# Four first-branch gate products moved from the S5 half steps to the Hyena convolutions of a hybrid block

## The chip, the cores and the metric

The kernel runs on one core of a Trainium2 chip. The metric is the device time of one execution in microseconds (us). The engines are named as in the profile: TensorE (PE; PEld is its weight load), VectorE (DVE), ScalarE (ACT), GpSimd (POOL) and SyncE (SP), which here only issues loads and stores.

## The reference

One layer of a diffusion backbone: 512 latent tokens and 256 context tokens, width 1024. The normalised, modulated tokens h are projected by one wide matrix to the inputs of three token mixers and to the merge gates. The parts that matter here, cut from the reference:

```
h = rmsnorm(x) * (1 + sc1) + sh1
k_l, v_l, a_l, u_l, q_l, r_l, hy_l, gate_l = split_cols(h @ w_in, COL_SIZES)
...
y_hy  = x2 * long_conv_bidir(x1 * long_conv_bidir(v, h0, h1), h2, h3)     # branch 0, two convolutions
y_gla = gated linear attention readout                                    # branch 1
y_s5  = s5_readout(s5_bidir(u_l ...))                                     # branch 2, complex diagonal states
m = sigmoid(g_hy) * (y_hy @ w_hy) + sigmoid(g_gla) * (y_gla @ w_gla) + sigmoid(g_s5) * (y_s5 @ w_s5)
x = x + gt1 * (m @ w_out)
x = x + gt2 * swiglu(rmsnorm(x) * (1 + sc2) + sh2)
```

All of it is float32. The S5 branch has 32 groups of channels; both directions are computed, and each block of four groups and one direction is a unit of work below.

## The kernel before

The order of the work is one list, STEPS, written out by hand (lines 366 to 595). Each engine walks the same list and does its own part of each step, in order, so a step that one engine waits in holds back all that stands behind it on that engine. Weights go through a ring of four slots of 1 MB: `want` puts a load into a plan, SP issues the loads in the plan's order, and load n is issued only when the last step that uses load n - 4 is done on PE. Weights of projections are used as a sum of two parts: ACT copies the rounded part (`split`, L1394) and POOL subtracts it (L1239), four pieces for each 1 MB block; a program places each block's split between the steps at the earliest place at which its two-slot ring is free.

A projection product (`merge_g`, `hy`) is 128 output channels by 512 tokens with 8 blocks of depth, each times three pairs of parts: 24 matmuls, at L695. A branch product (`merge_b`) is 4 plain float32 matmuls, which the trace shows as 8 records. Eight PSUM banks are used in turn: a product waits until the product eight before it has been evicted.

- `merge_g` of branch 0 ("kept" gates, k0 to k7): ACT takes the sigmoid and writes it to DRAM (`gate_spill`); it is read back behind the second convolution (POOL's `yinv`, L1299). DVE has no part in it.
- `merge_g` of branches 1 and 2 (g): ACT takes the sigmoid (`gate_ev`, L1560).
- `merge_b` (b): DVE multiplies by the gate and, for branch 2, adds into the sum (`merge_ev`, L2102, L2107).
- `hy` (h0 to h11): ACT scales (L1508), DVE adds the two neighbours of the short filter (`hy_ev`, L2120, L2121).

**S5's half steps** (lines 513 to 532). m runs from 0 to 15, two for each of 8 blocks. In half step m DVE turns the states of m (`s5_r`, with a scan at L2051), adds the kernel products of m + 1 (`s5_ka`, L2067 or L2069), turns back (`s5_x`, L2080 to L2083), makes the angles and factors of m + 2 (`s5_gen`, L1993 to L2008) and of its output (`s5_v`, L2021 to L2024). PE does the state products of m + 1 (`s5_d`, L919), in even half steps from 2 on the output products of the block before (`s5_y`, L945, L950), the transposes (`s5_w`, L906) and the kernel products of m + 2 (`s5_k`, L931), which wait for `s5_v`. `s5_v` of blocks 2 and up waits for the output products two blocks before. The last block's outputs stand behind half step 15. Two places in each half step take a filler from a list, `beside`: `one_beside` first does the eviction of the last filler product (all engines), then issues the next product. It is called once ahead of `s5_d` and once ahead of `s5_w`.

**The Hyena convolutions** (lines 546 to 562), cv = 0 and 1. PE transforms the tokens (`uspec`), DVE combines (`ubf`, L2198, L2199, with ACT's L1652), multiplies with the filter's spectrum (`ufilt`, L2209 to L2217), combines (`ucomb`, L2222, L2223), and PE transforms back (`yinv`), which waits for both `ucomb`. Fillers: one ahead of the first convolution, and in each convolution one behind each of the four `ufilt`, one ahead of `yinv` and one behind it. What is left in the list is done behind the second one, and then the eight branch products of branch 0.

```
def one_beside(more=True):
    if late:
        step(*late.pop(0))
    if beside and more:
        late.append(beside.pop(0)())
```

Of the kernel before, what the change touches and what calls it, by code (L numbers as in the profile page):

```python
# [67 lines left out]
def hybrid_block(nc, I, C, out):  # L68
# [31 lines left out]
    with es:  # L100
# [231 lines left out]
        def want(name, *parts, split=True):  # L332

            n, at, dmas, views = len(plan), 0, [], []
            s = (n % RS) * SLOT
            m = len(split_order)
            h = (m % HS) * SLOT
            for src in parts:
                k, w = src.shape[0] // P, src.shape[1]
                size = k * w  # L340
                dmas.append((v3(ring[:, s + at:s + at + size], k), src.rearrange("(k p) n -> p k n", p=P)))
                if split:
                    views.append((v3(ring_hi[:, h + at:h + at + size], k),
                                  v3(ring_lo[:, s + at:s + at + size], k)))
                else:
                    views.append(dmas[-1][0])
                at += size
            assert at <= SLOT
            cum[n % RS] += 16 * len(dmas)
            plan.append((name, dmas))  # L350
            if split:
                split_order.append(name)
            place[name] = (n % RS, cum[n % RS], views, at, m, len(plan) - 1)
# [4 lines left out]
        def step(*a):  # L358
            STEPS.append(a)
# [90 lines left out]
        def merge_steps(b):  # L450
            for jp in range(4):
                for h in range(2):
                    def unit(jp=jp, h=h):
                        if h == 0:
                            want(f"gate{b}{jp}", block(w_in, G0 + D * b + 256 * jp))
                        step("merge_g", b, jp, h)
                        return ("gate_ev" if b else "gate_spill", b, 2 * jp + h)
                    yield unit

                    def unit(jp=jp, h=h):  # L460
                        if h == 0:
                            want(f"br{b}{jp}", block(I[BR[b]][0], 256 * jp), split=False)
                        step("merge_b", b, jp, h)
                        return ("merge_ev", b, 2 * jp + h)
                    yield unit

        def hy_steps():
            for i in range(6):
                for h in range(2):
                    def unit(i=i, h=h):  # L470
                        if h == 0:
                            cols_slot(f"hy{i}", H0 + 256 * i)
                        step("hy", i, h)
                        return ("hy_ev", 2 * i + h)
                    yield unit

        ms, hy, kept = list(merge_steps(1)), list(hy_steps()), list(merge_steps(0))
        kept, ms0 = kept[0::2], kept[1::2]
        early, ms = ms[:6], ms[6:]
        beside = ms[:2] + hy[:2] + kept[:2] + ms[2:6] + hy[2:4] + kept[2:4] + hy[4:6] + ms[6:10] + hy[6:8] \  # L480
            + kept[4:6] + hy[8:10] + kept[6:8] + hy[10:12]
        late = []

        def one_beside(more=True):
# [4 lines that stand above are left out]
# [24 lines left out]
        for m in range(2 * NB):  # L513
            b, n = divmod(m, 2)
            step("s5_r", b, n)
            if m + 1 < 2 * NB:
                step("s5_ka", *divmod(m + 1, 2))
            one_beside()
            if m + 1 < 2 * NB:
                step("s5_d", *divmod(m + 1, 2))  # L520
            step("s5_x", b, n)
            if m + 2 < 2 * NB:
                step("s5_gen", *divmod(m + 2, 2))
            if n == 0 and b:
                step("s5_y", b - 1)
            if m + 2 < 2 * NB:
                step("s5_v", *divmod(m + 2, 2))
            one_beside()
            if m + 2 < 2 * NB:
                step("s5_w", *divmod(m + 2, 2))  # L530
                step("s5_k", *divmod(m + 2, 2))
# [4 lines left out]
        step("hy_tok")  # L536
        ms = list(merge_steps(2))
        evs = [ms[0](), ms[2]()]
        beside = [ms[1]] + ms[3:]
        want("glu", I["s5_w_glu"][0], split=False)  # L540
        step("s5_gelu")
        for e in evs:
# [21 lines left out]
        beside = ms0  # L564
# [1795 lines left out]
```

## Time and profile before

| what | value |
| --- | --- |
| runs of the kernel, median (lowest to highest) | 1300.87 us (1299.37 to 1303.38), 3 runs |
| the profiled execution | 1303.52 us, of which the span from first to last instruction 1301.7 us |
| busy share | PE 90%, DVE 45%, ACT 31%, POOL 31% |
| mean granted TensorE clock | 0.936 of 2.4 GHz |
| chain that ended last | PE 61%, DVE 11%, ACT 2%, issue 2%, DMA 1% |
| S5's half steps | 379 to 641 us |
| the two convolutions with their fillers | 684 to 812 us |
| branch 0's products | 812 to 839 us |

The chain that ended last is followed back from the last instruction, at each step to what released it. "idle ... <- X" says that the engine had nothing to run and that X's end released it. A granted clock of 1.00 is 2.4 GHz and 0.50 is 1.2 GHz; a value between them is a mixture over the stretch. Lines of records with the same shape are merged; x8 is the count.

### The profile page before, as it was taken

The page shows a single profiled execution, that of the slowest core. Times are in us where ns is not written, and L with a number is a line of the kernel's source. Part 1 is how long each engine was busy: PE and PEld are TensorE (multiplying, and loading weights), DVE is VectorE, ACT ScalarE, POOL GpSimd, SP SyncE. Part 2 cuts the span into 40 slices and gives each one's busy share as a digit, 9 for nine tenths or more (in the row PEclk, how much of TensorE's full clock was granted, in tenths as well). Part 3 has the DMA queues.
Part 4 walks back from the last instruction along what each step waited for, and adds up shares of the span by engine and source line. Part 5 has one row for each costly group of instructions (what it writes and reads, how often), then busy time and mean ns, then how long its engine had stood idle before and what let it go on. Part 6 is the DMA issues. An engine that isn't in the chain of part 4 may idle for free.

```text
span 1301.7 us, 15834 instructions
## 1 busy us (share of the span) xinstructions
PE 1177.5 (90%) x6157; PEld 889.3 (68%) x6157; DVE 579.4 (45%) x1081; ACT 405.1 (31%) x766; POOL 403.3 (31%) x339
## 2 busy tenths in 40 slices
PE   4689987966889999999898999998899999999995
PEld 1348955865658778678763556378788888888884
DVE  3594155556488788777205563634400012000013
ACT  1752312362344434443151110033333321233221
POOL 2012313420403133122131101043355554555541
PEclk9889988988989899898698999999999999999998
DMA  9702222574222323321161314655233223333211
GB/s 332 234 25 82 65 65 97 123 154 125 80 52 79 89 58 90 90 86 61 49 194 49 114 32 153 215 167 165 62 97 97 90 89 97 97 97 97 89 57 64
DMA packets 139862, 135.36 MB, mean 104 GB/s; under 512 B 13177, under 2 KB 126105, under 8 KB 138764
## 3 DMA queue, kind: packets, MB, share of 16 engines
q1 hardware_dynamic: 126432, 105.51, 27.8%
q0 software_dynamic: 4256, 17.20, 3.7%
q10 hardware_dynamic: 9100, 11.64, 2.9%
q8 instruction: 49, 0.80, 0.3%
q14 instruction: 25, 0.20, 0.0%
HBM read 121.23 MB, written 11.01 MB: 102 GB/s over the span
## 4 chain that ended last, share of the span: by engine, by line
PE 61%; DVE 11%; ACT 2%; issue 2%; DMA 1%; POOL 0%; ACTq 0%; DVEq 0%; POOLq 0%
PE psum L695 52%; PE psum L950 3%; PE psum L931 1%; PE psum L945 1%; PE psum L919 1%; DMA buf<-in_w_out 1%; DVE hT_lo L2285 1%; DVE buf L1874 1%; PE psum L906 0%; DVE buf L2222 0%; PE psum L861 0%; DVE buf L2324 0%; POOL ring_lo L1239 0%; DVE buf L2102 0%; DVE buf L2223 0%
## 5 line engine op out<-in xcount | busy, mean ns | idle before, releaser
L1239 POOL TENSOR_TENSOR ring_lo<-buf,ring_hi 128x512 fp32r<-128x512 f32 (+1 forms) x260 | 342.9, 1350 | 681.1 <-ACT ring_hi L1394 681.1
L695 PE MATMUL psum<-hT_hi,ring_hi 128*128 128x512 f32 x712 | 288.8, 406 | 5.4 <-DVE hT_lo L2285 4.0
L695 PE MATMUL psum<-hT_lo,ring_hi 128*128 128x512 f32 x712 | 282.1, 396 | 0.0
L695 PE MATMUL psum<-hT_hi,ring_lo 128*128 128x512 f32 x712 | 281.9, 396 | 0.0
L1394 ACT ACTIVATE ring_hi<-buf 128x512 fp32r<-128x512 f32 (+1 forms) x260 | 139.7, 610 | 233.9 <-PE psum L695 161.2
L695 PE MATMUL psum<-buf,buf 128*128 128x512 f32 (+1 forms) x448 | 196.8, 598 | 16.9 <-DVE buf L2174 6.6
L695 PEld LDWEIGHTS psum<-buf,buf 128*128 128x128 f32 x448 | 89.2, 202 | 115.0 <-issue 93.7
L695 PEld LDWEIGHTS psum<-hT_hi,ring_hi 128*128 128x128 f32 x712 | 136.8, 192 | 40.2 <-issue 6.4
L695 PEld LDWEIGHTS psum<-hT_hi,ring_lo 128*128 128x128 f32 x712 | 136.6, 192 | 29.6
L695 PEld LDWEIGHTS psum<-hT_lo,ring_hi 128*128 128x128 f32 x712 | 137.0, 192 | 28.8 <-issue 1.4
L2294 DVE TENSOR_TENSOR buf<-psum,buf 128x512 f32<-128x512 f32 x22 | 15.2, 692 | 220.9 <-PE psum L695 220.9
L695 PE MATMUL psum<-ring_hi,act_lo 128*128 128x512 f32 x176 | 69.6, 396 | 0.0
L695 PE MATMUL psum<-ring_lo,act_hi 128*128 128x512 f32 x176 | 69.6, 395 | 0.0
L695 PE MATMUL psum<-ring_hi,act_hi 128*128 128x512 f32 x176 | 69.6, 395 | 0.0
L2304 DVE TENSOR_TENSOR buf<-psum,buf 128x512 f32<-128x512 f32 x16 | 11.1, 691 | 99.5 <-PE psum L695 99.5
L950 PE MATMUL psum<-buf,buf 64*128 64x64 f32 x256 | 46.3, 336 | 0.0
L695 PE MATMUL psum<-ring_hi,hT_hi 128*128 128x256 f32 x128 | 37.1, 290 | 9.6 <-POOL ring_lo L1239 9.4
L950 PEld LDWEIGHTS psum<-buf,buf 64*128 64x128 f32 x256 | 41.2, 242 | 2.7
L695 PEld LDWEIGHTS psum<-ring_hi,act_lo 128*128 128x128 f32 x176 | 33.1, 188 | 8.0
L695 PEld LDWEIGHTS psum<-ring_lo,act_hi 128*128 128x128 f32 x176 | 33.1, 188 | 8.0
L695 PEld LDWEIGHTS psum<-ring_hi,act_hi 128*128 128x128 f32 x176 | 33.1, 188 | 8.0
L695 PE MATMUL psum<-ring_hi,mT_hi 128*128 128x256 f32 x128 | 36.6, 286 | 0.9 <-POOL ring_lo L1239 0.9
(319 smaller groups left out, 1670.5 us busy)
## 6 DMA issues: line engine op xcount, KB each, us to landing
buf<-in_w_in SPq DMA_DIRECT2D x26, 1024.0 KB, 5.3
buf<-in_w_mod SPq DMA_DIRECT2D x24, 1024.0 KB, 6.7
buf<-in_w_ffn_in SPq DMA_DIRECT2D x44, 512.0 KB, 5.3
buf<-in_w_ffn_out SPq DMA_DIRECT2D x8, 1024.0 KB, 5.1
scr_k<-buf POOLq DMA_DIRECT2D x4, 1024.0 KB, 5.2
buf<-scr_k POOLq DMA_DIRECT2D x4, 1024.0 KB, 8.7
buf<-in_w_out SPq DMA_DIRECT2D x4, 1024.0 KB, 5.2
buf<-in_w_ffn_out SPq DMA_DIRECT2D x4, 768.0 KB, 4.4
```

Source lines behind the costliest of these rows:

```text
L695: ins = nc.tensor.matmul(o, a, b, start=start and n == 0, stop=stop and n == len(pairs) - 1)
L919: ins = nc.tensor.matmul(o[s, ri, q, :], Wt[:, ri, q, s], U[:, GB * b + 2 * q + h, :], start=True, stop=True)
L931: ins = nc.tensor.matmul(banks[h][0:16, q * P:(q + 1) * P], Bb[d][1 + ri][s, 2 * b + q, :], V9[d][b % 2][s, ri, q, n:n + 8, :].rearrange(" ...
L945: nc.tensor.matmul(oo, Mt[b % 2][:, 2 * q + h, :], U[:, GB * b + 2 * q + h, NSC:NS], start=True, stop=False)
L950: ins = nc.tensor.matmul(oo, w, Xc[d][b % 2][s, ri, q, :], start=False, stop=n == 1 and ri == 1)
L1239: nc.gpsimd.tensor_tensor(ring_lo[:, a:a + n], ring[:, a:a + n], ring_hi[:, h + i * n:h + i * n + n].bitcast(fp32), SUB)\
L1394: A(ring_hi[:, h + i * n:h + i * n + n], ring[:, a:a + n], ACT.Copy).then_inc(S("w_hi"), 1)
L1874: ins = V.copy_predicated(am[:, u::2, :], mask[d].bitcast(i32).unsqueeze(1).to_broadcast([P, 2, P]), v3(o[:, 256 * n:256 * n + 256], 2))
L2285: V.tensor_tensor(hT_lo[:, k, :], hT[:, k, :], hT_hi[:, k, :].bitcast(fp32), SUB)\
L2294: V.tensor_tensor(actT[:, j % NFH, :], o, sA[j % 2], MUL).then_inc(freed(f"fb{j}"), 1)
L2304: V.tensor_tensor(xtmp, o, gt[1][:, c], MUL).then_inc(freed(name), 1)
```

## The change

The list of fillers for the S5 half steps loses the last four kept gates. The second filler place of every half step m with m % 3 == 2 issues no new product (it still does the eviction that is due). The list for the convolutions takes the four in.

```diff
         beside = ms[:2] + hy[:2] + kept[:2] + ms[2:6] + hy[2:4] + kept[2:4] + hy[4:6] + ms[6:10] + hy[6:8] \
-            + kept[4:6] + hy[8:10] + kept[6:8] + hy[10:12]
+            + hy[8:10] + hy[10:12]
@@
             if m + 2 < 2 * NB:
                 step("s5_v", *divmod(m + 2, 2))
-            one_beside()
+            one_beside(m % 3 != 2)
             if m + 2 < 2 * NB:
                 step("s5_w", *divmod(m + 2, 2))
@@
         ms = list(merge_steps(2))
         evs = [ms[0](), ms[2]()]
-        beside = [ms[1]] + ms[3:]
+        beside = [ms[1], ms[3]] + kept[4:6] + ms[4:8] + kept[6:8] + ms[8:]
```

Written out, the fillers of the half steps (g3 to g7 and b3 to b7 are branch 1's; a dash is an empty place):

| m | before | after | | m | before | after |
| --- | --- | --- | --- | --- | --- | --- |
| 0 | g3, b3 | g3, b3 | | 8 | g6, b6 | h4, - |
| 1 | h0, h1 | h0, h1 | | 9 | g7, b7 | h5, g6 |
| 2 | k0, k1 | k0, - | | 10 | h6, h7 | b6, g7 |
| 3 | g4, b4 | k1, g4 | | 11 | k4, k5 | b7, - |
| 4 | g5, b5 | b4, g5 | | 12 | h8, h9 | h6, h7 |
| 5 | h2, h3 | b5, - | | 13 | k6, k7 | h8, h9 |
| 6 | k2, k3 | h2, h3 | | 14 | h10, h11 | h10, - |
| 7 | h4, h5 | k2, k3 | | 15 | -, - | h11, - |

And of the convolutions (g2 to g7 and b0 to b7 are branch 2's; g0 and g1 are done ahead of them):

| place | before | after |
| --- | --- | --- |
| ahead of the first | b0 | b0 |
| first: four behind `ufilt`, one ahead of `yinv` | b1, g2, b2, g3, b3 | b1, k4, k5, g2, b2 |
| behind its `yinv` | g4 | g3 |
| second: four behind `ufilt`, one ahead of `yinv` | b4, g5, b5, g6, b6 | b3, k6, k7, g4, b4 |
| behind its `yinv` | g7 | g5 |
| left, ahead of branch 0's products | b7 | b5, g6, b6, g7, b7 |

The blocks' splits move with their products: in the half steps 12 blocks are split before and 10 after. In the plan of loads the block of k4 and k5 stands ahead of the block of g2 and g3, and the block of k6 and k7 ahead of the block of g4 and g5.

## Rows read from the trace of the kernel before

**Rows 1.** The page, section 4: the chain that ended last, by engine.
```profile
PE 61%; DVE 11%; ACT 2%; issue 2%; DMA 1%; POOL 0%; ACTq 0%; DVEq 0%; POOLq 0%
```
**Rows 2.** PE's waits (us in total, times, longest), half steps, last output, then convolutions.
```profile
PE psum L931 <- DVE buf L2024: 1.2, 3, 0.7
...
641.02 0.61 PE L945 MATMUL psum<-buf,buf 128*128 128x64 f32 x2 [4.01 <-DVE buf L2083]
...
PE psum L695 <- DVE buf L2102: 5.0, 1, 5.0
PE psum L695 <- DVEq L1712: 3.7, 2, 2.0
```
**Rows 3.** Stretches: length, busy PE, PEld, DVE, ACT, POOL (records), clock, DMA, GB/s.
```profile
404.20:424.90 20.70, 20.70 (x125) 16.93 (x125) 18.06 (x39) 8.29 (x18) 5.49 (x4) 0.92 0.26 74
...
459.20:472.80 13.60, 13.60 (x85) 10.77 (x86) 11.37 (x20) 6.43 (x13) 5.57 (x4) 1.00 0.25 80
...
614.60:637.00 22.40, 22.40 (x106) 18.28 (x104) 7.34 (x21) 5.22 (x12) 4.98 (x4) 0.77 0.18 54
637.00:651.10 14.10, 10.09 (x42) 9.14 (x42) 2.69 (x5) 0.96 (x2) 0.00 (x0) 0.65 0.25 76
...
788.60:801.00 12.40, 12.37 (x57) 10.92 (x58) 2.08 (x3) 0.00 (x0) 1.55 (x2) 1.00 0.48 169
```
**Rows 4.** The chain that ended last, half steps: start us, us, what.
```profile
385.49 3.63 PE psum L695 x8
...
389.56 0.98 PE psum L931 x16
390.54 5.68 PE psum L695 x24
...
416.43 7.04 PE psum L695 x24
...
522.73 6.51 PE psum L695 x8
...
620.27 0.81 PE psum L919 x16
...
628.70 8.33 PE psum L695 x24
```
**Rows 5.** The timeline of DVE in half steps 0, 2 and 4.
```profile
381.28 0.27 DVE L2069 TENSOR_TENSOR buf<-buf,psum 16x32 f32<-16x32 f32 x2
...
387.30 0.76 DVE L2024 TENSOR_TENSOR buf<-buf,buf 128x576 f32<-128x576 f32 x1
...
420.60 0.76 DVE L2024 TENSOR_TENSOR buf<-buf,buf 128x576 f32<-128x576 f32 x1
...
451.56 0.46 DVE L2021 TENSOR_TENSOR buf<-buf,buf 128x288 f32<-128x288 f32 x1 [7.05 <-PE psum L950]
```
**Rows 6.** The timeline of PE in the first convolution.
```profile
705.27 7.45 PE L695 MATMUL psum<-buf,buf 128*128 128x512 f32 x12 [4.97 <-DVE buf L2102]
...
726.93 3.59 PE L695 MATMUL psum<-buf,buf 128*128 128x512 f32 x8
```
**Rows 7.** The timeline of DVE in the first convolution.
```profile
717.64 0.69 DVE L2198 TENSOR_TENSOR buf<-psum,buf 128x512 f32<-128x512 f32 x1 [0.72 <-ACT buf L1652]
...
728.85 0.69 DVE L2107 TENSOR_TENSOR buf<-buf,buf 128x512 f32<-128x512 f32 x1
...
731.39 0.68 DVE L2223 TENSOR_TENSOR buf<-buf,buf 128x512 f32<-128x512 f32 x1
735.92 0.69 DVE L2232 TENSOR_TENSOR buf<-psum,buf 128x512 f32<-128x512 f32 x1 [3.85 <-PE psum L695]
```
**Rows 8.** The timeline of POOL and DVE beside a split, and DVE apart from one.
```profile
479.06 5.49 POOL L1239 TENSOR_TENSOR ring_lo<-buf,ring_hi 128x512 fp32r<-128x512 f32 x4 [12.56 <-ACT ring_hi L1394]
...
479.29 0.75 DVE L2121 SCALAR_TENSOR_TENSOR buf<-psum,buf,buf 128x511 f32<-128x511 f32 x1
...
699.87 1.75 DVE L2212 TENSOR_TENSOR buf<-buf,buf 128x512 f32<-128x512 f32 x1
...
721.75 0.68 DVE L2212 TENSOR_TENSOR buf<-buf,buf 128x512 f32<-128x512 f32 x1
```

## The prediction

> **What bounds the kernel now.** The page comes first: the chain that ended last is 61% TensorE (PE) and 11% VectorE (DVE), so a stretch is worth what PE does in it, unless PE waits for DVE there [rows 1]. The question is therefore who waits in the two stages that the change touches. The list of PE's waits answers: in S5's half steps (379 to 641 us) PE waited for DVE three times, 1.2 us in all, and once more, 4.01 us, ahead of the last S5 output; in the two convolutions (684 to 812 us) it waited 5.0 us for a PSUM bank and 3.7 us, twice, for DVE to finish the spectra [rows 2]. Both stages are close to balance between PE and DVE. The stretches by half step show the second limit, the clock: an even half step, which carries S5's output products, has a granted clock of 0.77 to 0.92, an odd one 1.00, and the last output 0.65 [rows 3]; TensorE is at 1.2 GHz for part of each even half step and at 2.4 GHz in the rest.
>
> The moved work cannot vanish: it is done on PE, at one place or at the other. What the change is worth is old idle time that goes, less new idle time that comes, and what the clock does. I call the four products k4 to k7, the order is in the table of the change.
>
> **S5: what leaves.** A gate product takes PE 5.68 us, a branch product 3.63, S5's state products 0.81, its kernel products 0.98 and the four transposes ahead of them about 0.5 (from 385.49 + 3.63 to 389.56) [rows 4]. Four gate products: 4 x 5.68 = **22.7 us**. The old idle in S5 is 1.2 + 4.0 = **5.2 us**. The 4.0 goes too: it was released by step x (L2083), which stood behind the eviction of the last Hyena product in an empty half step 15; now that product stands in half step 15 (5.68 us), DVE does x beneath it and the eviction after x.
>
> **S5: what idles next.** PE's kernel products of a half step wait for DVE's step v, and DVE starts from the kernel products of the half step before. Without a Hyena or branch eviction and without a split beside it DVE needs 6.5 us from its step ka (381.28 + 0.27) to the end of v (387.30 + 0.76) [rows 5], about 7.0 with the way from PE. The five thinned half steps, and two more:
> - 5 and 11 (a branch product alone, no split): PE has 3.6 + 0.8 + 0.5 = 4.9 us against DVE's 7.0; 2.1 us idle each, 4.2 together.
> - 2: the trace has this half step's DVE as it will be, up to v's end at 420.60 + 0.76 = 421.36 [rows 5]. PE is through with S5's output at 416.4 [rows 4], then 0.5 of transposes: 4.5 us idle.
> - 8: v is queued behind the end of the output products, as the row of half step 4 shows (DVE 7.05 us idle, released by L950) [rows 5]. v takes 2.35, the transposes 0.5 run beside it: 2.0 us idle.
> - 14: no later half step is prepared there, nothing waits: 0.
> - 7 and 13 keep two long products, a Hyena eviction and a split, the mix that now leaves some 0.2 (1.2 less 0.7, in two) [rows 2]: 0.4 together.
> New idle: 4.2 + 4.5 + 2.0 + 0.4 = **11.1 us**. Half steps 3 and 9 have their split in the second slot, behind v, where DVE has slack.
>
> **S5: the clock.** The last output (10.1 us busy in its stretch, clock 0.65) ran at 1.2 GHz, behind the 4.0 us idle [rows 3]. The same products behind busy work took 7.6 us in half step 14 (620.27 + 0.81 to 628.70) [rows 4]; I take 2.4 us off. After the 4.97 us wait in the convolution 12 records took 7.45 us, where 8 of the kind take 3.59 (the row at 726.93), so 5.4 at full clock: 2.1 us for one idle time of this length [rows 6]. I charge it once, for half step 2 (4.5 us); behind 2.0 us of idle the clock was 1.00 at 788.6 us [rows 3]. Sum for S5: 22.7 + 5.2 - 11.1 + 2.4 - 2.1 = **17.1 us gained**. (The Trainium skill, page TensorE: Matmul & The Clock Gate, section What's actually happening, speaks against thinning a stretch of TensorE: its clock halves when it has been idle and comes back only after sustained work. By that rule each of the new idle times could bring a fall, which is the third rival below.)
>
> **The convolutions: what arrives.** Of the four only k4 and k5 fall into the first convolution; k6 and k7 take slots of the second. The slots are no more than before, so each arrival pushes out a product of the third branch: five products are left behind the second convolution's inverse where one was. PE's work rises by 22.7, its old idle of 3.7 can be filled (the 5.0 wait for a bank comes ahead of the first moved product and stays). That is **19.0 us** if PE alone counts.
>
> DVE also counts. It runs through filter and combining steps from 717.6 to 732.1 us without a hole and PE stands waiting for it [rows 7]. Two things change. Gate products of the first branch have no DVE eviction, so one merge (L2102, L2107: 1.56 us) leaves the way to each spectrum. Against that, four weight splits run beside filter steps where one did, around 700 us: that one, k6/k7's block in the first convolution, and both later blocks of the third branch's gates in the second (one of them stood at the first inverse, where DVE had little to do). What a split does: beside GpSimd's part of it a filter operation takes 1.75 us, apart from it 0.68, and three are hit: 3.2 to 3.3 us for one split. A Hyena eviction (L2121), which reads PSUM, took 0.75 beside a split, not more than elsewhere [rows 8]. So filter and combining steps pay. (The Trainium skill, page SBUF — State Buffer, section Who interferes with whom, states just this division: a DVE instruction with two inputs in SBUF contends with GpSimd's reads, one with a single SBUF input doesn't. The trace agrees: 1.75 against 0.75.)
> - First: the block of k6 and k7 is split once k5's product is out, at about 724.5 on ACT and 725.6 to 731 on GpSimd, into the last filter step. DVE: 732.1 - 1.6 + 3.3 = 733.8. PE: 730.5 (726.93 + 3.59) + (5.68 - 3.4) = 732.8. Idle about 1.1.
> - Second: from inverse to inverse it was 788.6 - 732.2 = 56.4 us. PE needs 56.4 - 2.0 + 2.3 = 56.7. DVE: 56.4, less one merge 1.6, less 1.2 of small waits for PE that the slower filters cover, plus two splits 6.6 = 60.2. Idle about 3.6 (I take 3.7).
> New idle **4.8 us**; the convolutions cost 19.0 + 4.8 = **23.8 us**.
>
> Costed at nothing: SP loads the two moved blocks later, each when its ring slot is released, at the 4th entry ahead of it in the list of loads; the block of k4/k5 when half step 15's product ends and k6/k7's when the second branch product of the convolution ends, both 5 us or more ahead of their splits. S5's copies on SP keep their place behind step ka. ACT spills k7's gate some 10 us ahead of GpSimd's reload, and the reload itself now has 18 us more of PE work as cover; were it late, the first branch's merges would wait by what is missing, at most a few us.
>
> **Sum.** -17.1 + 23.8 = +6.7 us. The profiled execution took 1303.5 us, 2.6 above the median of the runs, so it gives 1310.2; at the median 1300.87 the forecast is **1307.6 us**.
>
> **Rivals.**
> - *The splits miss DVE's way* (they fall where DVE waits anyway). For it: DVE waited for the inverse for 3.9 us right behind the last combining step [rows 7], and a split a little later falls there. Against: ACT's order puts each split behind a gate eviction in mid filter. Then 19.0 - 17.1 = +1.9, 1302.8: no change. With S5's idle 2 us smaller, 1301. Chance 0.25.
> - *S5 pays in full.* Where a thinned even half step idles, it does so in its 1.2 GHz part: half steps 2 and 8 lost 1.4 and 2.9 us to that clock under their second product (7.04 and 6.51 us) [rows 4], and this would go too, with no fall after idle time. S5 then gains 17.1 + 2.1 + 4.3 = 23.5, the convolutions cost 19.0: 1296.4, faster. It decides if the splits also miss. Against: the first product of the next half step then stands in the low stretch. Chance 0.08.
> - *The clock falls at every new idle time.* 2.1 us after each of 5, 8 and 11 as well, and after both inverses' waits, while half step 14's low stretch runs on into half step 15: 5 x 2.1 = +10.5, 1318. For it: 0.77 in half step 14 [rows 3], and the 2.1 us lost at 705 us. Against: 2 us of idle kept full clock. One or two of these, 2 to 4 us, is likelier. Chance of the larger part 0.15.
> - *The change doesn't do what its words say:* half does not, since k6 and k7 go to the second convolution; the sum has that. If PE waited for DVE for long in the first, moving would be free; it waits 1.7.
>
> **How the numbers follow.** Forecast 0.52, rivals 0.25, 0.08, 0.15. A measurement of this kernel tells about 0.3% (3.9 us) from no change: slower is above 1304.8, faster below 1297.0. The forecast with its own errors (S5's idle times by 3 us, each split by 1) reaches 1302 to 1313, mostly above 1304.8; the third rival is slower, the first mostly the same. Slower 0.64, same 0.28, faster 0.08. The range takes in the first rival and half of the third: 1300.0 to 1315.5.
>
> **What would show it.** In the trace after: the start of the last S5 output 14 to 18 us earlier, with no idle ahead of it; idle of 2 to 5 us ahead of L931 in half steps 2, 5, 8 and 11; L1239 beside L2209 to L2217 four times instead of once; the second inverse 4 to 6 us later relative to the first weights of the glu product; 18 us more PE work between it and the first branch's products. It is wrong if S5's half steps shorten by 22 us or more, or if the filter steps show no 1.7 us operations.

## The result, and the profile after

The changed kernel took 1316.42 us at the median (1315.43 to 1317.37, 4 runs) against 1302.01 (1299.37 to 1303.38, 4 runs); the ratio is 1.0102, with an interval of 1.0086 to 1.0119. It is slower, as forecast, but by twice as much: 14.4 us where 6.7 were forecast, and outside the range (1300.0 to 1315.5).

The chain (page, section 4) is shown by engine and then by line; compare [rows 1]. DVE's filter steps L2209 to L2217 are among its first lines.

```profile
PE 62%; DVE 11%; issue 1%; ACT 1%; DMA 1%; POOL 0%; ACTq 0%; DVEq 0%; POOLq 0%
PE psum L695 53%; PE psum L950 3%; PE psum L931 1%; PE psum L945 1%; PE psum L919 1%; DVE buf L2214 1%; DMA buf<-in_w_out 1%; PE psum L724 1%; DVE buf L2209 1%; DVE hT_lo L2285 1%; DVE buf L2217 1%; DVE buf L2210 0%; DVE buf L2212 0%; DVE buf L2222 0%; DVE buf L2021 0%
```

PE's waits, in S5's half steps and then in the convolutions (us in total, times, longest), against [rows 2]: the 4.0 us ahead of the last output are gone, the waits for step v grew from 1.2 to 7.2 us (the later profiles of the same kernel have 9.5 to 9.8 us of waits here, see e1), those for the spectra from 3.7 to 7.9, and the wait for a bank stayed.

```profile
PE psum L931 <- DVE buf L2024: 7.2, 6, 1.9
...
PE psum L695 <- DVEq L1712: 7.9, 2, 5.5
PE psum L695 <- DVE buf L2102: 5.0, 1, 5.0
```

Stretches of the changed kernel, against [rows 3]: half steps 2, 5 and 14, the last output, and the second inverse (length, busy PE, PEld, DVE, ACT, POOL, granted clock, DMA share, GB/s). The last output has no idle time and takes 6.7 us. Half step 2 has a clock of 0.74 where it had 0.92. The second inverse, at 1.00 before, is at 0.80.

```profile
406.50:425.40 18.90, 17.43 (x102) 14.04 (x100) 16.84 (x34) 7.36 (x16) 5.50 (x4) 0.74 0.25 69
461.10:469.20 8.10, 6.16 (x46) 3.28 (x45) 7.30 (x20) 5.58 (x10) 0.00 (x0) 1.00 0.79 251
604.20:626.50 22.30, 22.30 (x106) 18.55 (x105) 13.83 (x29) 4.37 (x10) 5.50 (x4) 0.77 0.12 31
626.50:633.20 6.70, 6.70 (x42) 6.03 (x40) 1.50 (x2) 0.96 (x2) 0.00 (x0) 0.81 0.55 159
779.10:792.00 12.90, 12.88 (x48) 10.96 (x49) 1.38 (x2) 0.00 (x0) 1.54 (x2) 0.80 0.47 163
```

PE's timeline at half step 2's kernel products, the last output and the two inverses, to compare with [rows 2, 6]:

```profile
423.60 1.68 PE L931 MATMUL psum<-buf,buf 64*16 64x128 f32 x14 [1.47 <-DVE buf L2024]
...
626.53 0.33 PE L945 MATMUL psum<-buf,buf 128*128 128x64 f32 x2
...
717.20 14.00 PE L695 MATMUL psum<-buf,buf 128*128 128x512 f32 x32 [2.32 <-DVEq L1712]
...
779.12 1.22 PE L695 MATMUL psum<-buf,buf 128*128 128x256 f32 x2 [5.53 <-DVEq L1712]
```

And DVE and POOL beside the split of k6 and k7's block in the first convolution, to compare with [rows 7, 8]. Four operations are slow, not three, as many as GpSimd's subtraction has pieces (x4).

```profile
707.85 0.68 DVE L2212 TENSOR_TENSOR buf<-buf,buf 128x512 f32<-128x512 f32 x1
708.45 1.78 DVE L2214 TENSOR_TENSOR buf<-buf,buf 128x512 f32<-128x512 f32 x1
710.16 1.78 DVE L2215 TENSOR_TENSOR buf<-buf,buf 128x512 f32<-128x512 f32 x1
711.86 1.75 DVE L2217 TENSOR_TENSOR buf<-buf,buf 128x512 f32<-128x512 f32 x1
713.65 1.63 DVE L2222 TENSOR_TENSOR buf<-buf,buf 128x512 f32<-128x512 f32 x1
715.21 0.68 DVE L2223 TENSOR_TENSOR buf<-buf,buf 128x512 f32<-128x512 f32 x1
...
707.88 6.85 POOL L1239 TENSOR_TENSOR ring_lo<-buf,ring_hi 128x512 fp32r<-128x512 f32 x4 [23.09 <-ACT ring_hi L1394]
```

The stages over all profiles of the two kernels (three of before, four of the changed one; the later ones are from the experiments below), in us. The marks are the start of half step 0 (TensorE's first filler product there), the end of the last output, DVE's first L2198, its first operation behind each inverse (L2232, L2235), its last L2109, and the first L2284:

| stage | before | changed | difference of the means | forecast |
| --- | --- | --- | --- | --- |
| up to half step 0 | 378.9, 376.6, 377.0 | 381.4, 377.1, 378.7, 376.0 | +0.8 | 0 |
| half steps, last output | 272.1, 269.1, 272.2 | 251.7, 254.5, 254.5, 252.5 | -17.8 | -17.1 |
| to L2198 | 43.3, 43.3, 43.4 | 43.3, 43.4, 43.5, 43.4 | 0 | 0 |
| to the first inverse | 41.6, 41.3, 41.5 | 44.5, 44.5, 44.4, 45.5 | +3.2 | +1.7 |
| inverse to inverse | 56.5, 56.5, 56.6 | 64.5, 64.4, 64.4, 64.9 | +8.0 | +3.8 |
| to the last merge | 48.3, 48.3, 48.2 | 66.0, 66.0, 66.0, 66.0 | +17.7 | +18.3 |
| to the second norm | 75.3, 78.2, 75.6 | 78.7, 77.7, 77.7, 78.1 | +1.7 | 0 |
| the rest | 385.7, 386.1, 385.7 | 385.5, 385.8, 385.8, 385.9 | -0.1 | 0 |

By these means S5 gave back about what was forecast. The convolutions with what is left behind them cost 28.9 us, not 23.8. The rest, 2.4 us, lies in stages that the change does not touch. The four profiles of the changed kernel are all from its slower executions and the three of before from its faster ones (more on that below).

### The profile page after: what moved, and what is told of

Read it like the earlier page. It is cut to its first block, busy times and chain, and to the rows that moved or that the text cites. A ratio compares the mean times of both kernels' runs of the same rounds, so it can differ in the third digit from the quotient of the medians.

```text
span 1315.6 us, 15830 instructions
## 1 busy us (share of the span) xinstructions
PE 1188.1 (90%) x6157; PEld 900.6 (68%) x6157; DVE 582.7 (44%) x1081; ACT 401.7 (31%) x763; POOL 406.1 (31%) x339
## 4 chain that ended last, share of the span: by engine, by line
PE 62%; DVE 11%; issue 1%; ACT 1%; DMA 1%; POOL 0%; ACTq 0%; DVEq 0%; POOLq 0%
PE psum L695 53%; PE psum L950 3%; PE psum L931 1%; PE psum L945 1%; PE psum L919 1%; DVE buf L2214 1%; DMA buf<-in_w_out 1%; PE psum L724 1%; DVE buf L2209 1%; DVE hT_lo L2285 1%; DVE buf L2217 1%; DVE buf L2210 0%; DVE buf L2212 0%; DVE buf L2222 0%; DVE buf L2021 0%
## 5 line engine op out<-in xcount | busy, mean ns | idle before, releaser
L695 PE MATMUL psum<-hT_hi,ring_hi 128*128 128x512 f32 x712 | 290.7, 408 | 5.1 <-DVE hT_lo L2285 4.0
L695 PE MATMUL psum<-hT_lo,ring_hi 128*128 128x512 f32 x712 | 284.1, 399 | 0.0
L695 PE MATMUL psum<-hT_hi,ring_lo 128*128 128x512 f32 x712 | 283.7, 398 | 0.0
L695 PE MATMUL psum<-buf,buf 128*128 128x512 f32 (+1 forms) x448 | 193.7, 591 | 20.9 <-DVEq L1712 7.9
L695 PEld LDWEIGHTS psum<-buf,buf 128*128 128x128 f32 x448 | 89.0, 201 | 116.5 <-issue 91.1
L695 PEld LDWEIGHTS psum<-hT_hi,ring_hi 128*128 128x128 f32 x712 | 138.5, 195 | 40.0 <-issue 5.8
L695 PEld LDWEIGHTS psum<-hT_lo,ring_hi 128*128 128x128 f32 x712 | 138.4, 194 | 29.4 <-issue 1.4
L695 PEld LDWEIGHTS psum<-hT_hi,ring_lo 128*128 128x128 f32 x712 | 137.8, 193 | 30.0
L695 PE MATMUL psum<-ring_hi,act_lo 128*128 128x512 f32 x176 | 69.6, 396 | 0.0
L695 PE MATMUL psum<-ring_lo,act_hi 128*128 128x512 f32 x176 | 69.6, 395 | 0.0
L695 PE MATMUL psum<-ring_hi,act_hi 128*128 128x512 f32 x176 | 69.6, 395 | 0.0
L2304 DVE TENSOR_TENSOR buf<-psum,buf 128x512 f32<-128x512 f32 x16 | 11.1, 691 | 99.5 <-PE psum L695 99.5
L695 PE MATMUL psum<-ring_hi,hT_hi 128*128 128x256 f32 x128 | 37.4, 292 | 9.6 <-POOL ring_lo L1239 9.4
L695 PE MATMUL psum<-ring_hi,mT_hi 128*128 128x256 f32 x128 | 37.8, 295 | 3.9 <-POOL ring_lo L1239 3.9
L695 PEld LDWEIGHTS psum<-ring_hi,act_lo 128*128 128x128 f32 x176 | 33.1, 188 | 8.0
L695 PEld LDWEIGHTS psum<-ring_lo,act_hi 128*128 128x128 f32 x176 | 33.1, 188 | 8.0
L695 PEld LDWEIGHTS psum<-ring_hi,act_hi 128*128 128x128 f32 x176 | 33.1, 188 | 7.9
```

Of the source, the lines that this page charges most:

```text
L695: ins = nc.tensor.matmul(o, a, b, start=start and n == 0, stop=stop and n == len(pairs) - 1)
```

## The experiments

An edit that adds lines moves the line numbers behind it. Against the kernel before, the numbers in the rows shown are 1 higher in e7, 3 higher in e8, and in e3 and e6 3 higher from GpSimd's subtraction on (L2213 of e3 is L2210 of before) and unchanged ahead of it (L695).

**e1: the changed kernel again.** No edit.

> The changed kernel once more, with a second profile. In the first one the stretches outside the two stages were longer too: S5's half steps began 2.5 us later than in the profile of before (381.4 against 378.9) and the first output product 2.8 us later counted from the last merge. Theory A: both are part of the change; they come back within 0.5 us in this profile. Theory B: both are the phase at which the TensorE clock falls and rises, and differ from execution to execution; then at least one of them is off by more than 1 us here. The stages themselves repeat by both: half steps to the end of the last output 251.7 us, inverse to inverse 61.9 us, each within 1 us. Time 1316 us.

Measured: 1315.35 us median of 10, ratio 1.009 (1.0059 to 1.0121). Half step 0 began at 377.1 us, so that the 2.5 us of the first profile are not part of the change. The stage to the second norm was long again (77.7). Half steps 254.5 us, beyond the 1 us that was expected; inverse to inverse the same within 0.1. Theory B holds for the first, neither is shown for the second: with e5, 78.2 us stands in a profile of the kernel before too. PE's waits in the half steps differ from the first profile's as well:

```profile
PE psum L931 <- DVE buf L2024: 7.1, 6, 1.9
PE psum L906 <- DVE buf L2006: 2.4, 1, 2.4
```

The 2.4 us are in half step 2, ahead of its transposes. Its output products took 5.9 us here and 8.0 in the first profile, so TensorE came to the transposes earlier and waited there too: 2.4 + 1.4 = 3.8 us idle in half step 2, where the first profile has 1.5. The profiles of e9 and e10 have 3.8 and 3.7 as well. The idle time of the half steps is thus 7.2, 9.5, 9.5 and 9.8 us in the four profiles.

**e2, e11: the four products behind the last S5 output.** The half steps stay thinned.

```diff
         step("s5_y", NB - 1)
+        beside = kept[4:8]
         while late or beside:
             one_beside()
@@
-        beside = [ms[1], ms[3]] + kept[4:6] + ms[4:8] + kept[6:8] + ms[8:]
+        beside = [ms[1]] + ms[3:]
```

> S5's half steps exactly as in the changed kernel, but the four gate products k4 to k7 stand right behind the last S5 output, and the convolutions have the fillers of the kernel before. Theory (the moved work cancels, and the convolutions' price over 22.7 us is idle time of TensorE behind DVE's filter steps, the clock after it, and the splits): half steps 251.7 us as in the changed kernel; the convolutions take what they took before (inverse to inverse 56.4, idle ahead of it 2.0); the four products cost 22.7 less the 1.4 us that TensorE waited there; 1303 to 1306 us. Rival (the thinned half steps or the later stages hold the loss, wherever the four stand): 1312 us or more.

Measured: the profiled execution took 1304.5 us, but the median of 10 was 1316.52, with three executions at 1304 to 1306 and seven at 1315 to 1319 (below, the lower and the upper group). The convolutions were back at 41.0 and 56.1 us with no moved product in them, so their price belongs to what stands in them. The four products cost more than the 23.6 us that TensorE worked on them: ACT spills them in its order ahead of the token copies and the reload of S5's outputs, and PE then waited 6.9 us, until ACT had made the gate unit's input (L1534), where it had waited 1.4 us for the token copies. That is 28.8 us from the last output to L2198 (72.1 against 43.3): as dear as in the convolutions. The theory's sum (1303 to 1306) missed this wait, and neither side foresaw the two groups; by the median it is the rival's time (1312 or more), and the later stages do hold a part of the loss.

> The kernel with the four products right behind the last S5 output again, whose first profile was of its lower group (1304.5 us, half steps 244.6 us) while 7 of 10 executions took 1315 to 1319. Theory: a profile of the upper group has half steps of 251 to 255 us; the convolutions 41 and 56 us in either. Rival: the half steps stay at 245 and the 12 us are elsewhere.

Measured: 1317.9 us profiled, 1318.3 at the median of 7. The half steps of the two profiles (length, busy PE, PEld, DVE, ACT, POOL, clock), first of the one at 1304.5 us, then of the one at 1317.9:

```profile
376.40:621.00 244.60, 234.54 (x1389) 181.64 (x1385) 190.36 (x424) 92.33 (x192) 54.49 (x40) 0.90 0.26 72
```
```profile
377.30:631.90 254.60, 245.04 (x1389) 190.75 (x1385) 190.60 (x424) 92.58 (x192) 54.47 (x40) 0.86 0.25 69
```

The same instructions, DVE busy for the same time, and 10.0 of the 13.4 us between the two executions are in the half steps. (1 - 0.90) x 2 x 244.6 = 49 us of them were at 1.2 GHz in the one and 71 in the other (with the clock at two digits each is good to some 2.5 us); half of the 22 us, 11, is the time lost. The theory of the clock holds for this kernel. Of the other 3.4 us, 2.9 are in the two stretches behind (2.2 before the first L2198, 0.7 to the first inverse).

**e3: splits that read nothing.** The low part of the blocks of k6/k7, g4/g5 and g6/g7 is zeros and not computed.

```diff
                     a = s * SLOT + i * n
+                    if name in ("gate03", "gate22", "gate23"):
+                        nc.gpsimd.memset(ring_lo[:, a:a + n].bitcast(fp32), 0.0).then_inc(S("w_lo"), 1)
+                        continue
```

> The changed kernel, with the low part of three weight blocks (the one of k6 and k7, and the third branch's for g4 to g7) filled with zeros instead of computed, so GpSimd writes the same bytes but reads nothing; the low part of these eight gate products is left out. Theory (GpSimd's subtraction beside the filter steps slows DVE, and TensorE waits for it): the operations of 1.7 us in the filter steps are 0.7 us but for those at the one old split; idle ahead of the first inverse falls from 2.3 to under 0.5 us and ahead of the second from 5.5 to about 0.3; the clock stays up in the second inverse (2.5 us); 1307 to 1309 us. Rival (GpSimd's write slows DVE as much as its read, or DVE was not what TensorE waited for): within 2 us of the changed kernel, 1315.

Measured: 1302.31 us, 13.0 below the changed kernel in the same series and 5 below the 1307 to 1309 of the theory; ratio to before 0.9988 (0.9956 to 1.002). PE's waits in the convolutions, and DVE and POOL in the second one:

```profile
PE psum L695 <- DVE buf L2105: 5.0, 1, 5.0
PE psum L695 <- issue: 1.7, 1, 1.7
```
```profile
742.23 0.68 DVE L2213 TENSOR_TENSOR buf<-buf,buf 128x512 f32<-128x512 f32 x1
742.83 0.68 DVE L2215 TENSOR_TENSOR buf<-buf,buf 128x512 f32<-128x512 f32 x1
...
741.20 2.02 POOL L1240 MEMSET ring_lo<- 128x512 f32 x4 [28.37 <-ACT ring_hi L1397]
```
```profile
716.90:773.00 56.10, 56.10 (x185) 34.74 (x184) 30.82 (x49) 8.83 (x16) 5.56 (x10) 1.00 0.24 81
```

No wait for the spectra is left, the clock stays at 1.00, and the stages are 42.0 and 56.1 us: 2.7 and 8.4 less than in the changed kernel. So three splits beside filters cost 11.1 us on the path, the lower clock behind their longest wait among them, and without them the eleven places up to the second inverse, four moved gates among them, take the time they took before; only the 17.7 us behind them remain, against 19.3 that the half steps gave back here (251.8). A zero fill also takes a third of the subtraction's time, 2.0 against 6.3 us, so the read and the shorter time are not told apart as the cause; a memset that lay beside a 0.68 us operation did not slow it at all. The half steps of this profile are those of the changed kernel's slower executions, clock and all:

```profile
379.90:631.60 251.70, 244.43 (x1387) 190.41 (x1385) 189.57 (x422) 92.19 (x190) 54.28 (x40) 0.87 0.25 68
```

**e4: the last Hyena product in half step 15, nothing moved.**

```diff
-            one_beside()
+            one_beside(m != 14)
```

> The kernel before with one edit: the second filler of half step 14 is left empty, so the last Hyena product stands in half step 15, and nothing is moved to the convolutions. Theory (of the 20.4 us that the half steps lost in the changed kernel, the 4.0 us of idle ahead of the last output and 3.5 us of its half clock come from half step 15 alone, and thinning the others returned only 13 for 22.7): 7 to 8 us faster than before, 1294 to 1296 us, idle ahead of the last output 0, the output 6.5 us instead of 10.0. Rival (the gain comes from thinning as such): within 2 us of the kernel before.

Measured: 1296.26 us, ratio 0.9954 (0.9931 to 0.9977): 5.9 us under the kernel before. Half steps 266.8 us against 271.1. The last output began without idle time (the rows of PE's timeline have no wait in them):

```profile
640.33 0.33 PE L945 MATMUL psum<-buf,buf 128*128 128x64 f32 x2
640.59 1.10 PE L950 MATMUL psum<-buf,buf 64*128 64x64 f32 x8
```

By the medians the theory holds with 1 to 2 us less than it expected. The profiled execution, 3 us above the median, has a wait of PE in half step 8 that no profile of before has; ACT there issues S5's eight copies (3.9 us) and then evicts the gate that PE's bank waits for:

```profile
PE psum L695 <- ACT buf L1560: 3.2, 1, 3.2
PE psum L931 <- DVE buf L2024: 1.2, 3, 0.8
```

The profiles of e7 and e8 have the same half steps without that wait, and take 264.6 and 264.7 us. So of the changed kernel's 17.8 us some 6.5 come from half step 15 alone, and the thinned places returned some 11 for 22.7 us of work.

**e5, e12: the kernel before again.** No edit.

> The kernel before once more, with a second profile, so that each stage has two of either kernel. Theory (the stages repeat but for the clock): half steps to the end of the last output 272 us within 5, last evictions to the first inverse 41.6 and inverse to inverse 56.5 within 0.5; the half steps' share of time at 1.2 GHz differs from the first profile's by some us, and so does their length, by half of it. Rival (the stages repeat within 1 us, clock and all): 272.1 us again.

Measured: 1303.18 us median of 10. Half steps 269.1 us, 59 us of them at 1.2 GHz (65 in the first profile, 272.1): 6 us and 3 us, the half as the theory says. 41.3 and 56.5 us in the convolutions.

> The kernel before, third profile. Theory: half steps 269 to 272 us where it takes 1300 to 1304, 276 to 279 us where it takes 1310 to 1312; the convolutions 41.5 and 56.5 us in either.

Measured: 1302.0 us profiled, 1302.86 at the median of 8, half steps 272.2, convolutions 41.5 and 56.6. No profile of the unedited kernel before is of its upper group, so that theory is not tested on it. The nearest is e6's profiled execution (below), 1308.1 us, of that kernel's upper group of 1307 to 1310: its half steps took 276.7 us, but 3.2 of them are the wait for ACT that e4's profile has. So it does not test the theory cleanly either.

**e6: one split of the kernel before that reads nothing.** As e3, for the block of g4 and g5 alone, in the kernel before.

> The kernel before, with the low part of one weight block (the one split at 696 us, for the third branch's g4 and g5) filled with zeros instead of computed; this low part is left out of those two gate products. It prices one split beside one filter step by itself. Theory (4 us for each split): DVE's first filter step has no 1.7 us operation, and the first inverse starts 3 to 4 us earlier counted from the first L2198, 1298 to 1299 us. Rival (the bank wait of 5.0 us and PE's products set the first inverse, DVE's delay is hidden): less than 1 us.

Measured: 1299.71 us median against 1303.18 of e5 in the same series, 3.5 less. From the first L2198 to the first inverse 36.1 us, 5.4 less; but inverse to inverse 58.2, 1.7 more. The bank wait fell too, since its release stands behind the filter step on DVE:

```profile
PE psum L695 <- DVEq L1715: 3.7, 2, 2.0
PE psum L695 <- issue: 1.7, 1, 1.7
PE psum L695 <- DVE buf L2105: 1.5, 1, 1.5
```

The rival (under 1 us) is out. DVE itself loses 3.5 us to this split, and the bank wait fell by just that, 5.0 to 1.5. The other 1.9 us and the 1.7 that went the other way are the clock. Ahead of the first inverse it was 0.92 before and 1.00 here; at the second inverse it was 1.00 before and here it fell, behind the same 2.0 us of idle:

```profile
699.50:735.60 36.10, 32.92 (x99) 18.36 (x98) 29.45 (x46) 7.14 (x13) 5.50 (x8) 1.00 0.25 77
788.30:793.80 5.50, 5.46 (x17) 4.52 (x18) 0.01 (x1) 0.00 (x0) 1.54 (x2) 0.69 0.64 217
```

**e7: e4's edit, and the first merge ahead of the transform.**

```diff
         step("glu")
         one_beside()
+        one_beside(False)
```

> The kernel before with the last Hyena product in half step 15, and the first branch product of the third branch merged right behind its product, ahead of the first transform, instead of behind the first filter step. Nothing moves between the stages. Theory: the PSUM bank that TensorE waited 5.0 us for at 700 us is free, the merge (1.6 us) is off DVE's way and DVE does not wait 3.1 us for the next product; the first inverse comes 4 to 5 us earlier counted from the first L2198, so 11 to 12 us less than the kernel before, 1290 to 1292 us. Rival (DVE's filters alone set the inverse): 1.6 us less than with the Hyena product alone, 1295.

Measured: 1294.52 us, ratio 0.9915 (0.9881 to 0.9949); the rival said 1295, the theory 1290 to 1292. The bank wait is gone; the wait for the spectra took its place:

```profile
PE psum L696 <- DVEq L1713: 6.1, 2, 4.4
PE psum L696 <- issue: 1.7, 1, 1.7
```

The first inverse came 2.8 us earlier (38.4 against 41.2 in e4), between theory and rival, nearer to the rival by the time: DVE's filters, one of them beside a split, are the bound behind the bank.

**e8: both, and the split of g4 and g5's block ahead of the first transform.** Everything is computed.

```diff
+            if name == "gate22":
+                at = STEPS.index(("uspec", 0, 0))
             assert at <= first_use[name], name
```

> As the one with both edits, and the split that ran beside the first filter step (the block of g4 and g5) is put ahead of the first transform, where DVE has nothing to do. Everything is computed. Theory: DVE's 1.7 us operations in the first filter step are gone, another 3 to 4 us off the way to the first inverse, 1287 to 1289 us. Rival (the load of that block lands too late, or TensorE's products now set the inverse): under 1.5 us gained.

Measured: 1290.04 us, ratio **0.9893 (0.9843 to 0.9944)**, 13 us less than the kernel before in the same series (1303.4). It is the median of 4, a little above the 1287 to 1289 of the theory. PE's waits in the convolutions, and two operations of the first filter step (L2212 and L2214 of before, at 1.75 us there) with the split that now lies ahead of it:

```profile
PE psum L698 <- DVEq L1715: 3.4, 2, 1.7
PE psum L698 <- issue: 1.7, 1, 1.7
```
```profile
688.98 0.69 DVE L2215 TENSOR_TENSOR buf<-buf,buf 128x512 f32<-128x512 f32 x1
689.58 0.69 DVE L2217 TENSOR_TENSOR buf<-buf,buf 128x512 f32<-128x512 f32 x1
...
679.45 5.39 POOL L1242 TENSOR_TENSOR ring_lo<-buf,ring_hi 128x512 fp32r<-128x512 f32 x4 [12.49 <-ACT ring_hi L1397]
```

34.4 us to the first inverse, 4.0 less than e7: the wait ahead of it fell from 4.4 to 1.7 us, and the clock of the stretch rose from 0.96 to 1.00.

**e9, e10: the changed kernel, third and fourth profile.**

> The changed kernel unedited, for a third profile (the two next runs give a fourth and one of the other kernel). Its executions fall into two groups, 1306 to 1310 and 1315 to 1317 us (3 and 11 of 14), those of the kernel before into 1297 to 1304 and 1310 to 1312 (mostly the first); both profiles of the changed kernel were of its upper group. Theory (the groups are the phase of the TensorE clock against S5's even half steps, and differ in how long the half steps run at 1.2 GHz; between like groups the change costs 5 to 7 us): a profile near 1306 us shows half steps of 244 to 248 us and up to 50 us of them at half clock, one near 1316 us 251 to 255 us and 65 to 71 us, with the convolution stages equal within 0.5 us. Rival (the groups come from another place, loads or stages outside S5): half steps of 252 to 255 us in both.

> The same again, with the same expectation: if this profile is of the other group than the last, the two are compared stage by stage; if not, it is one more sample of how long the half steps run at 1.2 GHz.

Measured: both profiled executions were of the upper group (1316.8 and 1314.1 us, half steps 254.5 and 252.5, at half clock 71 and 66 us); the medians were 1314.99 and 1315.61, of 8 each. So the changed kernel has no profile of the lower group, and the comparison rests on e2 and e11, which share its half steps. Over all its runs, 6 of 30 executions of the changed kernel took under 1311 us (1304.2 to 1310.4) and 24 took 1314 to 1318. In e10 the clock also fell behind the wait of 2.3 us ahead of the first inverse, which took 5.5 us to its first result, 1.7 more than in the other three profiles, where it was 1.00 there:

```profile
711.90:717.40 5.50, 5.47 (x9) 2.39 (x10) 0.03 (x1) 0.00 (x0) 1.09 (x2) 0.69 0.71 261
```

## Why the prediction was right or wrong

- **What leaves S5 (22.7 + 5.2 us): right.** TensorE's work in the half steps, counted at full clock, is 22.4 us less, the idle ahead of the last output vanished, and e4 shows this part alone.
- **New idle in the half steps (11.1 us): right in kind, 2 us too much.** The four profiles have 7.2, 9.5, 9.5 and 9.8 us, 9.0 in the mean. Half steps 5 and 11 had 1.9 us where 2.1 were forecast, half step 8 had 1.5 to 1.8 for 2.0. Half step 2 had 3.8 for 4.5 in three profiles and 1.5 in the first, whose output products there ran at half clock (8.0 us instead of 5.9), beneath which DVE caught up.
- **The clock in S5 (+2.4 - 2.1): 1 us too little charged.** The last output did run in 6.7 us instead of 10.1. By the clock's records over the profiles the half steps had 68.7 us at half clock against 62.4, but 4.8 of the 68.7 fell into idle time and cost nothing; half of the remaining difference is 0.8 us lost, where 0.3 gained were forecast. 22.4 + 5.2 - 9.0 - 0.8 = 17.8, which is what was measured; forecast 17.1. That the number is so near is partly luck: two errors of opposite sign, and e2's profile shows the same half steps in 244.6 us, 26.5 less than before.
- **The step that failed: "three are hit: 3.2 to 3.3 us for one split".** The old split cost 3.5 us: three operations at 1.75 us, and the 0.94 us of the one ahead of them was read as nothing. The three new ones hit four operations, 0.7 to 1.1 us each: 3.9 to 4.2 us for a split. With 4.2 the forecast's own sums give 732.1 - 1.6 + 4.2 = 734.7, 1.9 us idle ahead of the first inverse (measured 2.3), and 56.4 - 2.8 + 8.4 = 62.0 us from inverse to inverse (measured 779.1 - 717.2 = 61.9), 5.3 us idle (measured 5.5). That is 2.4 us. (The Trainium skill, page SBUF — State Buffer, section Who interferes with whom, calls the pair of ports that the two engines share an exclusive lock. The traces fit it: four GpSimd instructions, four slow operations. Counting the instructions would have given nearly the right number.)
- **The second term of the same step: the clock behind that idle.** It was only in the third rival, at 2.1 us. The wait of 5.5 us brought the second inverse to half clock in all four profiles, 2.5 us. Behind the 2.3 us ahead of the first inverse the clock stayed up in three profiles, as the forecast said, and fell in e10's (1.7 us there). So the convolutions cost 19.0 + 1.9 + 5.3 + 2.5 = 28.7; measured 28.9. The forecast had 23.8. Its ground for charging nothing, "2 us of idle kept full clock", was one row: e6's profile lost the clock behind the same 2.0 us at the same place. In these traces an idle time of 2.0 to 2.3 us sometimes costs the clock and sometimes does not.
- **The splits as the cause: shown** by e3 (11.1 us on the path for three, in both inverses, the 2.5 us of clock among them) and e6 and e8 (one). The first rival, that they miss DVE's way, is out.
- **What the forecast did not have: two groups of executions.** The kernel before takes mostly 1297 to 1307 us and sometimes 1309 to 1313 (19 of its 101 runs), the changed one mostly 1314 to 1318 and sometimes 1304 to 1310 (6 of 30). Set side by side by rank, the upper groups differ by 4 us (1315.9 against 1311.9 and 1312.1 at the medians of two series), the lower ones by 4.5 in one series (1306.3 against 1301.8) and 0.6 in the other (1304.4 against 1303.9), with three executions of the changed kernel in each. So much of the 14.4 us between the medians is that the changed kernel falls into its upper group four times in five. That the groups differ by S5's time at 1.2 GHz is shown for one kernel (e2 and e11). e3 has the changed kernel's half steps and seems to have both groups too: 2 of its 10 executions took 1296 to 1297 us, the other 8 took 1301 to 1305, and the profiled one of these has the upper group's 251.7 us of half steps. Why the thinned half steps fall into the upper group so often, and whether a group of one kernel is the same thing as that of another, is open.
- **Open:** 0.8 us ahead of the half steps and 1.7 behind the last merge. Profiles of before and of other kernels cover the same values (75.2 to 78.5), so that chance can explain them, but nothing tells it apart.

## What to carry to other kernels

Moving filler work between two balanced stages is worth only the idle time that it removes; here one product into the empty half step 15 gave 5.9 us alone, and with four more moved to the other stage the kernel was 14 us slower. When a step is moved, look for what is tied to it: the weight split on GpSimd, not the product, was what the forecast undercharged, and in these traces it goes by instructions, one slow operation on VectorE for each of GpSimd's. A step with two SBUF inputs on VectorE's critical way wants its neighbours' splits ahead of it, in time in which VectorE waits for TensorE (e8: 4 us for one).

## What the runs showed of the hardware

A zero fill on GpSimd (2.0 us for four pieces) lay beside VectorE's two-input operations and left them at 0.68 us, where a subtraction of the same size made them 1.75 us and itself took 6.3 instead of 5.0 to 5.6. (This is what the Trainium skill says on the page SBUF — State Buffer, section Who interferes with whom: a GpSimd instruction that only writes does not contend with a VectorE instruction with two SBUF inputs.) The clock behind a short idle time was not the same in every execution: 1.00 in three profiles and 0.69 in one behind 2.3 us, 1.00 before and 0.69 in e6 behind 2.0 us; behind 5.5 us it fell in all four. And one and the same program had 49 or 71 us at 1.2 GHz in one stage, by execution, with 10 us of difference: a single profile says which group it is from only beside the times of the other runs.
